# Experts of a hybrid Hyena and attention layer: GpSimd takes part of the low halves, the gather moves, the ring's slots are freed by the products

## The reference, cut to what matters

```python
def _expert_choice(h, router, w_gate, w_up, w_down):
    cap = EC_CAPACITY * L // N_EXPERTS                 # 2 * 1024 // 16 = 128 tokens
    aff = jax.nn.softmax((h @ router).astype(jnp.float32), axis=-1)
    g, idx = lax.top_k(jnp.swapaxes(aff, 1, 2), cap)   # per expert its 128 tokens
    ...
    xin = h[bidx, idx_flat].reshape(B, N_EXPERTS, cap, D)
    a = jnp.einsum('becd,edf->becf', xin, w_gate)      # D = 1024, D_FF = 2048
    b = jnp.einsum('becd,edf->becf', xin, w_up)
    y = jnp.einsum('becf,efd->becd', jax.nn.silu(a) * b, w_down)
    y = (y * g[..., None].astype(y.dtype)).reshape(B, N_EXPERTS * cap, D)
    return jnp.zeros_like(h).at[bidx, idx_flat].add(y)
```

## Time and profile before

| | |
|---|---|
| median of 3 runs | 2219.31 us (2218.79 to 2220.83) |
| profiled execution | 2220.32 us |
| its span, first to last instruction | 2218.2 us |
| mean granted TensorE clock | 0.982 of 2.4 GHz |
| TensorE / VectorE / ScalarE / GpSimd busy | 96 / 75 / 52 / 9% of the span |
| moved by DMA | 538 MB, 243 GB/s on average |

### The profile page before, as it was taken

How to read it: one execution, slowest core, us unless ns; L and a number is a source line. 1 busy time by engine, 2 the same in 40 slices (tenths; PEclk the granted TensorE clock), 3 DMA queues, 4 the chain that set the end, 5 groups by cost and what they waited for, 6 DMA issues and landing times.

```text
span 2218.2 us, 27445 instructions
## 1 busy us (share of the span) xinstructions
PE 2123.9 (96%) x10117; PEld 1707.5 (77%) x10117; DVE 1668.3 (75%) x1720; ACT 1160.6 (52%) x1229; POOL 191.5 (9%) x69
## 2 busy tenths in 40 slices
PE   7999999989999999999399999999999999999998
PEld 2998888866577776688278888888888888888886
DVE  3657765267654898763789888998989889898986
ACT  3521222156400221331177777777777777777774
POOL 0000000000000000400011101101101111011100
PEclk9999999999999999999699999999999999999999
DMA  8134354030120132653489999999999999999993
GB/s 308 51 104 161 130 190 156 38 129 15 20 77 12 64 114 90 224 180 125 179 323 363 380 393 394 381 378 380 389 398 383 379 377 378 400 388 381 379 379 116
DMA packets 183292, 538.34 MB, mean 243 GB/s; under 512 B 15231, under 2 KB 57355, under 8 KB 182708
## 3 DMA queue, kind: packets, MB, share of 16 engines
q1 hardware_dynamic: 172768, 505.67, 60.8%
q0 software_dynamic: 4752, 16.78, 2.9%
q10 hardware_dynamic: 5700, 14.90, 1.7%
HBM read 501.66 MB, written 35.65 MB: 242 GB/s over the span
## 4 chain that ended last, share of the span: by engine, by line
PE 49%; DVE 2%; DMA 0%; issue 0%; ACT 0%; POOL 0%; POOLq 0%
PE p_y L248 5%; PE p_y L250 5%; PE p_a L248 5%; PE p_a L250 5%; PE p_a L249 5%; PE p_y L249 5%; PE p_b L250 5%; PE p_b L249 5%; PE p_b L248 5%; PE p_t L2463 1%; PE p_t L2454 1%; DVE idx_rows L2418 1%; DVE late L2421 0%; DVE vals L2416 0%; DMA g1row<-xn_dram,idx_e 0%
## 5 line engine op out<-in xcount | busy, mean ns | idle before, releaser
L2359 DVE TENSOR_TENSOR r_lo<-ring,r_hi 128x2048 fp32r<-128x2048 f32 x384 | 865.7, 2286 | 63.0 <-ACT r_hi L2318 56.0
L2318 ACT ACTIVATE r_hi<-ring 128x2048 fp32r<-128x2048 f32 x384 | 731.2, 1916 | 154.4 <-PE p_b L250 75.4
L248 PE MATMUL p_y<-r_hi,a_hi 128*128 128x512 f32 x512 | 205.3, 401 | 0.0
L248 PE MATMUL p_a<-r_hi,x_hi 128*128 128x512 f32 x512 | 202.5, 396 | 1.0 <-DVE x_lo L2370 1.0
L250 PE MATMUL p_y<-r_hi,a_lo 128*128 128x512 f32 x512 | 200.0, 391 | 0.0
L250 PE MATMUL p_a<-r_hi,x_lo 128*128 128x512 f32 x512 | 199.8, 390 | 0.0
L249 PE MATMUL p_a<-r_lo,x_hi 128*128 128x512 f32 x512 | 199.2, 389 | 0.0
L249 PE MATMUL p_y<-r_lo,a_hi 128*128 128x512 f32 x512 | 199.2, 389 | 0.0
L248 PE MATMUL p_b<-r_hi,x_hi 128*128 128x512 f32 x512 | 199.2, 389 | 0.0
L249 PE MATMUL p_b<-r_lo,x_hi 128*128 128x512 f32 x512 | 199.2, 389 | 0.0
L250 PE MATMUL p_b<-r_hi,x_lo 128*128 128x512 f32 x512 | 199.2, 389 | 0.0
(11 more groups left out here) (352 smaller groups left out, 3640.4 us busy)
## 6 DMA issues: line engine op xcount, KB each, us to landing
ring<-in_w_gate SPq DMA_DIRECT2D x128, 1024.0 KB, 8.5
ring<-in_w_up SPq DMA_DIRECT2D x128, 1024.0 KB, 8.2
ring<-in_w_down SPq DMA_DIRECT2D x128, 1024.0 KB, 12.0
w_raw<-in_w_in SPq DMA_DIRECT2D x17, 1024.0 KB, 6.2
ada_rest<-in_ada_w SPq DMA_DIRECT2D x16, 1024.0 KB, 5.4
ada<-in_ada_w SPq DMA_DIRECT2D x8, 1024.0 KB, 15.4
gate_dram<-zs ACTq DMA_DIRECT2D x16, 512.0 KB, 2.6
x_normed<-gate_dram SPq DMA_DIRECT2D x16, 512.0 KB, 4.2
```

The costliest lines, as they stand in the source:

```text
L248: pe.matmul(out, a_hi, b_hi, start=start, stop=False)
L2318: act.activation(r_hi[:, i % PARTS], ring[:, i % RAW], ACT.Copy).then_inc(hi_ready, 1)
L2359: dve.tensor_tensor(r_lo[:, i % PARTS], ring[:, i % RAW], r_hi[:, i % PARTS].bitcast(F32), ALU.subtract).then_inc(lo_ready, 1)
```

## The change

Three things are done, all in the experts:

1. In the 16 units 3 to 10 and 16 to 23 of each expert (`SHARED`), VectorE subtracts only columns 0 to 1279, and GpSimd columns 1280 to 2047, into the same slot of `r_lo`. GpSimd's part has a semaphore of its own, `lo_far_ready`, for which TensorE waits too.
2. GpSimd issues the gather for the next expert in step 8 of its body, between its part of unit 10 and that of unit 16. Before it stood at the start of the body, right behind the add of the expert before. The add stays at the end of the body.
3. SP refills a slot of the ring once the products of the unit in it are done (`unit_done`), no longer when the low part is made. `lo_ready` alone would not cover the reads of GpSimd.

```diff
--- before.py
+++ after.py
@@ -81,6 +81,9 @@
 EU = GU + FF // 256
 RAW, PARTS = 12, 4
 AHEAD = 3
+NEAR_LOW = 1280
+SHARED = [i for i in range(EU) if i >= AHEAD and not 11 <= i <= 15]
+GATHER_AT = 8
 TURNS = 6
 TURN_AT = {8: 0, 9: 1, 16: 2, 17: 3, 19: 4, 20: 5}
 
@@ -2244,6 +2247,7 @@
         as_float, turned, kept = sem("as_float"), sem("turned"), sem("kept")
         mirror_zero, mirror_ready, lists_ready, mirrored = sem("mirror_zero"), sem("mirror_ready"), sem("lists"), sem("mirrored")
         hi_ready, lo_ready, unit_done = sem("hi_ready"), sem("lo_ready"), sem("unit_done")
+        lo_far_ready = sem("lo_far_ready")
         idx_ready, gathered, gate_ready = sem("idx_ready"), sem("gathered"), sem("gate_ready")
         turn, turn_f, turn_hi, turn_lo = sem("turn"), sem("turn_f"), sem("turn_hi"), sem("turn_lo")
         silu_ready, au_ready = sem("silu_ready"), sem("au_ready")
@@ -2265,7 +2269,7 @@
                         if first and i < 4:
                             continue
                         if not (first and i < RAW):
-                            sp.wait_ge(lo_ready, EU * e + i - RAW + 1)
+                            sp.wait_ge(unit_done, EU * e + i - RAW + 1)
                         load_unit(sp, g, e, i)
                 each_expert(sp, body)
 
@@ -2290,9 +2294,17 @@
 
                 halves = g["out"][0].rearrange("t (h n) -> (t h) n", h=2)
 
+                def low_part(e, i):
+                    pool.wait_ge(hi_ready, EU * e + i + 1)
+                    pool.tensor_tensor(r_lo[:, i % PARTS, NEAR_LOW:], ring[:, i % RAW, NEAR_LOW:],
+                                       r_hi[:, i % PARTS, NEAR_LOW:].bitcast(F32), ALU.subtract).then_inc(lo_far_ready, 1)
+
                 def body(e, first, last):
-                    if not last:
-                        gather(e + 1)
+                    for i in range(EU):
+                        if i + AHEAD in SHARED:
+                            low_part(e, i + AHEAD)
+                        if i == GATHER_AT and not last:
+                            gather(e + 1)
                     if not first:
                         pool.wait_ge(added, 16 * e)
                     pool.wait_ge(yo_ready, e + 1)
@@ -2356,8 +2368,9 @@
             def _(dve):
                 def low_part(e, i):
                     dve.wait_ge(hi_ready, EU * e + i + 1)
-                    dve.tensor_tensor(r_lo[:, i % PARTS], ring[:, i % RAW], r_hi[:, i % PARTS].bitcast(F32),
-                                      ALU.subtract).then_inc(lo_ready, 1)
+                    at = slice(0, NEAR_LOW if i % EU in SHARED else 2048)
+                    dve.tensor_tensor(r_lo[:, i % PARTS, at], ring[:, i % RAW, at],
+                                      r_hi[:, i % PARTS, at].bitcast(F32), ALU.subtract).then_inc(lo_ready, 1)
 
                 def take_index(e, first):
                     if not first:
@@ -2466,6 +2479,8 @@
                 def body(e, first, last):
                     for i in range(EU):
                         pe.wait_ge(lo_ready, EU * e + i + 1)
+                        if i in SHARED:
+                            pe.wait_ge(lo_far_ready, shared_until(e, i))
                         hi, lo = r_hi[:, i % PARTS], r_lo[:, i % PARTS]
                         if i < GU:
                             c, q = divmod(i, 2 * HU)
@@ -2487,6 +2502,7 @@
                             if h == 0:
                                 pe.wait_ge(turn_lo, turns(e, (i - GU) // 2))
                                 pe.wait_ge(lo_ready, EU * e + EU)
+                                pe.wait_ge(lo_far_ready, shared_until(e, EU - 1))
                             for k in range(4):
                                 kk, slot = FF // P - 4 + k, (EU - 2 + k // 2) % PARTS
                                 at = slice(D * (k % 2) + 512 * h, D * (k % 2) + 512 * h + 512)
@@ -2534,6 +2550,11 @@
                 each_expert(pe, body)
 
 
+def shared_until(e, i):
+
+    return len(SHARED) * e + sum(u <= i % EU for u in SHARED) - (len(SHARED) if i < 0 else 0)
+
+
 def turns_before(e):
 
     return TURNS * e + 2
```

## The result

The changed kernel takes 2306.83 us (median of 4 runs, 2305.04 to 2309.83) against 2219.25 us: ratio 1.0395, 95% interval 1.0382 to 1.0408. The direction was forecast, the size was not: 87.6 us more instead of 46. Its profiled execution took 2309.83 us with a span of 2307.7, 89.5 us over the span before.

The account below looks back on a forecast made before the run. TensorE's products bound the experts, so nothing could be gained; 15 experts x 3.0 us plus 0.5 for the first, added to 2220.3 us profiled, gave 2265.8, median 2265 us; range 2243 to 2298.

Parts of the forecast that it names:

- the pair: Shared unit: GpSimd's 1.69 us and VectorE's 1.36 us in turns, sum 3.05 us against TensorE's 2.72.
- The slots: Ring of loads: a slot is released 6.4 us later, which leaves 11 us; cost 0.
- the moved gather: GpSimd's gather between its parts of units 10 and 16: 1.35 to 8 us, none on the path.
- The second stretch: Units 16 to 23: the low parts fit with 2 us left, so no second loss.
- Then the chain in turns.: Units 3 to 10: VectorE and GpSimd alternate on low parts; unit 10 begins 3.0 us late, 45 us over 15 experts.
- rival (a): VectorE is served first, GpSimd gets in only at its gaps: 5.0 us an expert, +75, 2294; chance 0.12.
- Unit 3: First shared unit of an expert: GpSimd comes late from the add, so TensorE gets it 2.4 us late.
- From unit 3 to unit 10: First shared stretch of an expert: TensorE's lateness grows from 2.4 us to 3.0 us.
- The ends: First expert: no add ahead and 2 us in hand, 0 to 1 us, taken as 0.5.
- rival (b): Engines side by side, add still in the way at unit 3: 0.9 to 2.2 us x 15, 2234 to 2252; chance 0.08.
- a hold of GpSimd's whole 1.82 us: Shared unit by the skill's lock rule taken literally: 3.18 us a unit, and the 45 us become about 60.

Follow-up runs that it names:

- experiment 5: Changed kernel, but only GpSimd's part of unit 4 waits for the end of its part of unit 3; 2270.45 us, ratio 1.0234 to the kernel before.
- experiment 1: Changed kernel with no unit shared, only the gather in step 8 and the later release of slots left; 2219.73 us, ratio 1.0001 to the kernel before.
- experiment 10: Changed kernel with sharing only in units 6 to 10 and 16 to 23 of each expert; 2222.34 us, ratio 1.0011 to the kernel before.
- experiment 2: Changed kernel with sharing only in units 16 to 23 of each expert; 2220.18 us, ratio 1.0005 to the kernel before.
- experiment 4: Changed kernel, but GpSimd waits for the end of its own last part before each next one; 2271.72 us, ratio 1.0239 to the kernel before.
- experiment 6: Changed kernel with an expert's add issued behind GpSimd's part of unit 3 of the next expert; 2277.83 us, ratio 1.0264 to the kernel before.
- experiment 8: Changed kernel with VectorE's share raised to 1536 columns and GpSimd's cut to 512; 2271.83 us, ratio 1.0239 to the kernel before.

## Why the prediction was wrong in size

Right: TensorE is the bound, so nothing could be gained. GpSimd and VectorE take turns on operations with two SBUF inputs; the pair was priced at 3.05 us and measured 3.06 (experiment 5). The slots cost nothing (experiment 1), nor does the moved gather (experiment 10). The second stretch costs nothing (experiment 2). No loss after unit 10.

Wrong, by the steps of the sum:

- **The step that failed: "Then the chain in turns."** I let the two engines change over after almost every operation, because the merge stage showed that the earlier trace rows. With the row of GpSimd's parts behind the add they don't. VectorE's part of unit 5 waited for five of GpSimd's. It is the mirror image of rival (a), in which I had only VectorE shut GpSimd out; no rival had this. Worth 72.95 - 71.27 = 1.68 us in 15 experts, 25 us.
- **The clock.** Not in the forecast. 9 x 1.28 = 11.5 us, gone together with the shutting-out in experiments 4 and 5. What makes the clock fall in some experts and not in others isn't settled: experiment 6 had a wait of 2.9 us in each expert and no fall, experiment 8 one of 2.5 us and seven falls.
- **Unit 3** was taken as 2.4 us late and was 1.2: GpSimd's part was asked for at t = 6.92, while the add still ran (I had the add end first and 0.3 us pass), and it was GpSimd's turn at 7.45, when VectorE's part of unit 4 ended, ahead of VectorE's part of unit 5. 18.5 us instead of 36.
- **From unit 3 to unit 10** I had 0.6 us; experiment 5 shows 71.27 - 68.11 - 1.23 = 1.9, of it 0.34 to 0.42 in each of the units 3 to 7. I had let GpSimd run two parts in a row where it suited the sum. 29 us instead of 9. The two errors cancel, so 71.1 us an expert was close to the 71.27 without the shutting-out, partly by luck.
- **The ends.** The first expert 2.9 us (I had 0.5) and 0.9 us ahead of it, which is not the change's: the first expert began between 1115.9 and 1120.6 us over all the runs here. The last 1.8 us: TensorE asks there for the parts of the last two units at once, a wait of 1.7 us in experiments 2 and 10 too.

The sum in the span: 18.5 + 29 + 25 + 11.5 + 3.8 + 1.8 = 89.6, measured 89.5 (2307.7 - 2218.2). One reading of the prediction is off besides: its range, from 2243 up, takes in half of rival (b), 2234 to 2252, and not most of it.

The Trainium skill, "SBUF — State Buffer" (the section on the two sides of SBUF), has it that whichever engine begins first keeps the shared pair for the whole instruction and the other is fully blocked. The runs agree that none of a pair's work overlaps, but the pair took 3.06 us, as priced in turns, and not the 3.18 that the prediction worked out for a hold of GpSimd's whole 1.82 us. And they show 10.25 us for an operation of 1.48 us, so here the block lasted over five instructions, which the sentence doesn't let one expect.

## What to carry to other kernels

Read first whether the relieved engine is one that somebody waits for; here TensorE never had, and every helper could only add waits. If GpSimd takes part of a two-input VectorE operation, price the pair as the sum of both, and look for the place where GpSimd comes late: it is there, with a row of parts ready, that VectorE can be kept out for the whole row. TensorE's lead hid five such units in experiment 10 and eight in experiment 2, so where the sharing began mattered more than how much was shared. And see in the trace that an experiment isolates what it is meant to: an instruction that stands in step 8 of the code needn't run at that time (experiment 1).

## What the runs showed of the hardware

- Behind an indirect DMA's issue, GpSimd's subtractions of 768 columns began 1.8 us apart, each 0.2 us before the end of the one ahead, and VectorE's two-input subtraction waited for all of them (10.25 and 8.70 us against 1.48; five and four of them). One wait of GpSimd on its own semaphore brought the overlap down to 0.04 us and VectorE got in after each (3.10 us). No run here shows the reason.
- The other way round, two of VectorE's subtractions of 1536 columns in a row kept GpSimd's 512 columns waiting (3.60 us against 1.3) in twelve of 15 experts of experiment 8, and not in three.
- The issue of an indirect DMA on GpSimd took 7.96 us behind a row of VectorE's 2048-column subtractions (experiment 1) and 2.08 us on average in the changed kernel. The row alone doesn't decide it: in the kernel before one gather, at 1468.65, took 1.35 us beside a row of five subtractions (11.27 us from 1466.87) like the one beside which the gather at 1536.76 took 7.96 (11.27 us from 1534.98).
- GpSimd's next subtraction began 0.5 us before the issue of the add ended (1566.93 against 1567.47).
- TensorE's clock was granted at 0.50 for 3.4 us in nine experts of the changed kernel, after two waits of 1.1 and 2.8 us, and in seven of experiment 8, after one of 2.5 us. In the six other experts of the one that had both waits, in five of the other and in experiment 6, with a wait of 2.9 us in each expert, it did not fall.
